# Both MLP products of the second block as seven half-size products of sums of quarters, and a weight ring of four slots

## What is computed

```python
def squared_relu_mlp(h, w_ff1, w_ff2):
    return jnp.square(jax.nn.relu(h @ w_ff1)) @ w_ff2

    for l in range(DEPTH_2):
        ...
        h2 = modulate(rms_norm(x_lat, g_mlp[l]), sh2, sc2)
        x_lat = x_lat + gt2 * squared_relu_mlp(h2, w_ff1[l], w_ff2[l])
```

## Time and profile before

| | |
|---|---|
| three runs, us | 4598.55, 4602.85, 4605.67; median 4602.85 |
| profiled execution, us | 4597.72, its span 4596.0 |
| granted clock of TensorE, mean | 0.928 of 2.4 GHz |
| first MLP product (L342), both layers | 1024 matmuls, 439.9 us |
| second MLP product (L2960), both layers | 1024 matmuls, 439.9 us |
| TensorE / VectorE / ScalarE busy, us | 4005.6 / 1115.7 / 728.0 |

### The profile page before, as it was taken

How to read it: one execution, slowest core, us unless ns; L and a number is a source line. 1 busy time by engine, 2 the same in 40 slices (tenths; PEclk the granted TensorE clock), 3 DMA queues, 4 the chain that set the end, 5 groups by cost and what they waited for, 6 DMA issues and landing times. The chain is left out here.

```text
span 4596.0 us, 36789 instructions
## 1 busy us (share of the span) xinstructions
PE 4005.6 (87%) x14604; PEld 2114.7 (46%) x14604; DVE 1115.7 (24%) x2442; ACT 728.0 (16%) x1623; POOL 166.5 (4%) x374
## 2 busy tenths in 40 slices
PE   8986886997689999999366989999997698989999
PEld 3653853443443445554144554444445455444443
DVE  0148524112222111112224350211001435021000
ACT  0213111000122110001013340110002334010000
POOL 1010000000100000000103000000000300000000
PEclk9987886998699999999688999999998899999999
DMA  7432012223366677887421111222222111221221
GB/s 275 176 127 101 1 41 83 80 85 120 131 267 256 274 296 308 349 315 298 152 61 55 37 37 55 100 83 73 92 68 87 55 37 37 73 110 55 75 103 42
DMA packets 200480, 582.93 MB, mean 127 GB/s; under 512 B 22116, under 2 KB 37780, under 8 KB 187304
## 3 DMA queue, kind: packets, MB, share of 16 engines
q1 hardware_dynamic: 186040, 542.94, 31.9%
q0 software_dynamic: 7184, 23.91, 1.4%
q10 hardware_dynamic: 7088, 13.73, 0.8%
HBM read 545.68 MB, written 34.88 MB: 126 GB/s over the span
## 5 line engine op out<-in xcount | busy, mean ns | idle before, releaser
L342 PE MATMUL ps<-ring,layer_hT 128*128 128x512 f32 (+2 forms) x1632 | 621.1, 540 | 7.9 <-PEq L272 7.9
L342 PEld LDWEIGHTS ps<-ring,layer_hT 128*128 128x128 f32 x1632 | 306.0, 196 | 313.7 <-issue 307.2
L2960 PE MATMUL ps<-ring,mlp_hidden 128*128 128x512 f32 x1024 | 439.9, 592 | 3.2 <-PEq L272 3.2
L342 PE MATMUL ps<-layer_hT,ring 128*128 128x512 f32 x1024 | 439.9, 592 | 1.9 <-PEq L272 1.9
L342 PE MATMUL ps<-ring,mixers_xT 128*128 128x512 f32 (+3 forms) x992 | 372.5, 532 | 9.4 <-DVE ab_qk L336 6.0
L2960 PEld LDWEIGHTS ps<-ring,mlp_hidden 128*128 128x128 f32 x1024 | 194.4, 190 | 248.8 <-issue 248.8
L342 PEld LDWEIGHTS ps<-layer_hT,ring 128*128 128x128 f32 x1024 | 194.4, 190 | 246.3 <-issue 246.3
L342 PEld LDWEIGHTS ps<-ring,mixers_xT 128*128 128x128 f32 x992 | 188.6, 200 | 187.3 <-issue 174.1
L342 PE MATMUL ps<-mixers_xT,ring 128*128 128x512 f32 (+2 forms) x560 | 188.4, 496 | 1.9 <-DMA ring<-in_w_ff 1.0
L2032 PE MATMUL ps<-ring,moe_xgT 128*64 128x512 f32 x320 | 144.4, 607 | 2.9 <-issue 2.9
L342 PEld LDWEIGHTS ps<-mixers_xT,ring 128*128 128x128 f32 (+1 forms) x560 | 104.0, 187 | 84.0 <-issue 74.7
(11 more groups left out here) (734 smaller groups left out, 4974.2 us busy)
## 6 DMA issues: line engine op xcount, KB each, us to landing
ring<-in_w_ff SPq DMA_DIRECT2D x40, 2048.0 KB
ring<-in_w_in SPq DMA_DIRECT2D x33, 2048.0 KB
ring<-in_e_up SPq DMA_DIRECT2D x21, 2048.0 KB
ring<-in_w_ada SPq DMA_DIRECT2D x18, 2048.0 KB
ring<-in_e_down SPq DMA_DIRECT2D x18, 2048.0 KB
ring<-in_e_gate SPq DMA_DIRECT2D x18, 2048.0 KB
ring<-in_w_out SPq DMA_DIRECT2D x8, 2048.0 KB
mixers_ring_more<-in_e_gate SPq DMA_DIRECT2D x8, 2048.0 KB, 9.3
```

What stands on the lines that cost most here:

```text
L342: last = pe.matmul(out, lhsT, rhs, start=(j == 0), stop=(j == len(pairs) - 1))
L2960: last_ = pe.matmul(M.ps[:, bank_of(half, t), :], hidden[:, k * DK + j, t * P:(t + 1) * P], w[:, j, :], start=(k == 0 and j == 0), stop=(k ...
```

## The change

Both products are done in Winograd's form of Strassen's scheme. With A and B cut into quarters (11, 12, 21, 22) the sums are S1 = A21 + A22, S2 = S1 - A11, S3 = A11 - A21, S4 = A12 - S2 and R1 = B12 - B11, R2 = B22 - R1, R3 = B22 - B12, R4 = B21 - R2. The products, by their numbers in the code, are 1 = A11 B11, 2 = A12 B21, 5 = S1 R1, 6 = S2 R2, 7 = S3 R3, 3 = S4 B22 and 4 = A22 R4, issued in this order. The result is C11 = 1 + 2, C12 = 1 + 6 + 5 + 3, C21 = 1 + 6 + 7 + 4 and C22 = 1 + 6 + 7 + 5. All sums are made on VectorE.

*First product* (`first_product`): a pair of weight tiles (1024 x 1024) is A, and `hT` is B, cut at 512 features and 256 tokens. Each of the seven products is two groups (x = 0, 1); a group has 2 x 4 products of 256 moving columns. S of each pair is made on VectorE from the tiles (128 x 2048 elements an operation), R once a layer from `hT` (128 x 1024). ScalarE evacuates products 1 and 5; VectorE evacuates the rest, adds the parts and makes relu and square in one scalar_tensor_tensor. There are four pairs.

*Second product* (`second_product`): a part is 1024 hidden features, with `hidden` as A and two tiles of `w_ff2` (1024 rows x 512 columns each) as B. Each of the seven products is two groups of 4 products with 512 moving columns. The seven products of the four parts are accumulated in SBUF: part 0 is copied there by ScalarE, parts 1 to 3 are added by VectorE. In the last part the results are combined, scaled and added to the rows behind each product. The rows are loaded from ScalarE's queue after part 0, into `hidden`'s space, and each is saved from there as soon as it is done. The sums S are 128 x 1024 elements, R 128 x 2048.

*Ring:* `RING` is 4 and the extra slot of the first block goes, so the first block has four slots and the experts five, as before, and the second block four in place of three. The spare experts' up-weights go to the buffer `loose` of the context instead of a slot. The order of the tiles of `w_ff2` follows the parts.

```diff
-RING = 3
+RING = 4
...
-    wg, wu = M.weights.bufs[RING:RING + 2]
+    wg, wu = M.weights.bufs[RING], loose[:, 0:TILE]
...
-        for half in range(2):
-            for k in range(4):
-                tiles += weight_tiles(A["w_ff2_2"][l, k * D:(k + 1) * D], half * BANK, (half + 1) * BANK)
+        for k in range(4):
+            tiles += weight_tiles(A["w_ff2_2"][l, k * D:(k + 1) * D], 0, D)
...
+def left_sum(i, link, eng, bufs, a11, a12, a21, a22):
+    one, two = bufs
+    if i == 1:
+        return eng.tensor_tensor(one, a21, a22, ALU.add)
+    if i == 2:
+        return eng.tensor_tensor(two, one, a11, ALU.subtract)
+    if i == 3:
+        return eng.tensor_tensor(one, a11, a21, ALU.subtract)
+    return eng.tensor_tensor(two, a12, two, ALU.subtract)
...
+def first_product(M, name, hT, hidden, sums):
...
+    def product(p, x, left, right, ev, on, needs, after=()):
+        def pe(pe_, bank):
+            for h in range(2):
+                c = (2 * x + h) * P
+                last = matmuls(pe_, bank[:, h * rows:(h + 1) * rows],
+                               [(left[:, j, c:c + P], right[:, j, :]) for j in range(half)])
+            return last
...
+    def square(dve, out):
+        return dve.scalar_tensor_tensor(out, out, 0.0, out, ALU.max, ALU.mult)
+
+    def left(p, i, reads, after=()):
+        def ev(dve, _, link):
+            if i == 1:
+                W.arrived(dve, t0 + 2 * p)
+                W.arrived(dve, t0 + 2 * p + 1)
+            return left_sum(i, link, dve, S, *a(p))
+        return group(None, ev, "v", reads=reads, after=after)
...
+        p2 = [product(p, x, a12, b[2], lambda dve, bank, link, p=p, x=x: c11(dve, bank, link, p, x), "v", (),
+                      (p1[x],)) for x in range(2)]
+        p5 = [product(p, x, S[0], R[0], lambda act, bank, link, p=p, x=x: act.activation(
+            dst(p, x, 1, 1), bank, ACT.Copy), "s", (s1, r1)) for x in range(2)]
+        gs += p1 + p2 + p5
+        s3 = left(p, 3, (p5[1],), (s2,))
...
+def second_product(M, name, hidden, hT, gt, sums, last):
...
+        def add(n, x, left, right, needs, then=None, after=()):
+            v = V[n, x]
+
+            def ev(eng, bank, link, k=k):
+                if k == 0:
+                    return move(eng, v, bank)
+                total = eng.tensor_tensor(v, v, bank, ALU.add)
...
+        both("1", a11, b11, ())
+        both("2", a12, b21, (), c11, lambda x: (now["1", x], loaded[x]))
+        both("5", S[0], R[0], (s1, r1))
+        s3, r3 = left(k, 3, (now["5", 1],), (s2,)), right(k, 3, (now["5", 1],), (r2,))
+        gs += [s3, r3]
+        both("6", S[1], R[1], (s2, r2), u2, lambda x: (now["1", x], now["5", x], before["3", x]))
+        s4, r4 = left(k, 4, (now["6", 1],)), right(k, 4, (now["6", 1],))
+        gs += [s4, r4]
+        both("7", S[0], R[0], (s3, r3), c22, lambda x: (now["6", x], before["4", x], loaded[2 + x]))
...
+        both("3", S[1], b22, (s4,), c12, lambda x: (now["6", x],))
...
+        both("4", a22, R[1], (r4,), c21, lambda x: (now["7", x],))
...
 def mlp(M, L, l, hT, last):
...
-        products(M, f"ff1_p{l}", gs, tiles=8)
...
+        first_product(M, f"ff1_{l}", hT, hidden, sums)
+        second_product(M, f"ff2_{l}", hidden, hT, gt, sums, last)
```

More of the change, by code:

```diff
@@ L2024, in experts @@
         sc = st.ctx.enter_context(Stage(nc, "ctx"))
-        sections, load_ctx = context_sections(M, sc, lambda i: index["ctx", i])
+        sections, load_ctx, loose = context_sections(M, sc, lambda i: index["ctx", i])
         filler = by_slot(sections, places, 2 * pairs)
@@ L2108, in experts, with spare_experts @@
             spare_experts(M, sr, route, slot_rows, idx, xg[:, 0, :], xgT[:, 0, :, :], sg[:, 0, :], h[:, 0, :],
[L2109 to L2112 removed]
+                          hT[:, 0, :], y[:, 0, :], loose)
+def spare_experts(M, st, route, slot_rows, idx, xg, xgT, sg, h, hT, y, loose):
     nc, A, sig, ds = M.nc, M.A, st.sig, bass.ds
     done = st.sb("done", [1, 1])
[L2120 removed]
+    wg, wu = M.weights.bufs[RING], loose[:, 0:TILE]
     wd = M.xT[:, :, :].rearrange("p k n -> p (k n)")
@@ L2905, in squared_relu, with right_sum @@
     return ev
+def left_sum(i, link, eng, bufs, a11, a12, a21, a22):
[7 more added lines that the diff above has]
+    return eng.tensor_tensor(two, a12, two, ALU.subtract)
+def right_sum(i, link, eng, bufs, b11, b12, b21, b22):
+    one, two = bufs
+    if i == 1:
+        return eng.tensor_tensor(one, b12, b11, ALU.subtract)
+    if i == 2:
+        return eng.tensor_tensor(two, b22, one, ALU.subtract)
+    if i == 3:
+        return eng.tensor_tensor(one, b22, b12, ALU.subtract)
+    return eng.tensor_tensor(two, b21, two, ALU.subtract)
@@ L2913, in mlp @@
         gt = st.sb("gt", [P, D])
+        sums = st.sb("sums", [P, 9 * BANK * 2])
         products(M, f"gt2_{l}", gate_row_groups(M, L.mod, 5 * DK, 0, gt))
[L2915 to L2919, removed]
-        products(M, f"ff1_p{l}", gs, tiles=8)
-        x = hT[:, :, :].rearrange("p k n -> p (k n)").rearrange("p (t d) -> p t d", d=D)
@@ L2923, in mlp @@
[L2923 to L2959, removed]
-                                last_ = pe.matmul(M.ps[:, bank_of(half, t), :],
-                                                  hidden[:, k * DK + j, t * P:(t + 1) * P], w[:, j, :],
-                                                  start=(k == 0 and j == 0), stop=(k == 3 and j == DK - 1))
-                            if k == 3 and t < TT - 1:
-                                last_.then_inc(sig["summed"], 1)
-                        last_.then_inc(W.groups_done, 1)
-            @block.vector
-            def _(dve):
-                link = Chain(dve, sig["chain"])
-                dve.wait_ge(sig["x"], 16 * TT)
-                for half in range(2):
-                    for t in range(TT):
-                        if t < TT - 1:
-                            dve.wait_ge(sig["summed"], half * (TT - 1) + t + 1)
-                        else:
-                            dve.wait_ge(W.groups_done, base + 4 * half + 4)
-                        ev(dve, M.ps[:, bank_of(half, t), :], link, t, half).then_inc(sig["moved"], 1)
@@ L3231, in context_sections @@
     sections += [ks + nk_work, vs + nk_turned + near_saves]
-    return sections, load
+    return sections, load, ins
 def by_slot(sections, places, slots):
@@ L3321, in program @@
             tiles += [t] + turns[2 * j:2 * j + 2]
-        slots = [RING + 1] * len(tiles)
+        slots = [RING] * len(tiles)
         for n in range(4):
@@ L3362, in program @@
         with Stage(nc, "mixers") as st:
-            M.weights.bufs.append(st.sb("ring_more", [P, TILE])[:, :])
             M.ones = st.sb("ones", [P, P])
```

161 lines of the change are left out of this document (added).

## The result

The changed kernel takes 4484.17 us (median of four runs, 4481.17 to 4488.25) against 4600.7 for the kernel before, run beside it (four runs, 4590.02 to 4605.67): ratio 0.975, 95% interval 0.9731 to 0.977. The forecast was 4491, its range 4479 to 4513. A second set of runs gave 4486.03 (five runs) against 4595.25 (nine runs), ratio 0.9757 (0.9743 to 0.9772). Between the profiled executions, whose terms the forecast added up, the spans went from 4596.0 to 4486.5: -109.5 us, where -111.6 was forecast.

The account below looks back on a forecast made before the run. TensorE bounds both MLP products, by number of matmuls times spacing. Terms -107.9 - 2.1 + 0.4 - 2.0 = -111.6 us against the profiled 4597.72 give 4486.1; with 5.1 to the median, 4491, range 4479 to 4513.

Parts of the forecast that it names:

- First product, -26.5 a layer: First MLP product: 896 matmuls of 256 columns at 0.2158 us, 193.5 us a layer against 219.97.
- Second product, -27.5 a layer: Second MLP product: 448 matmuls of 512 columns at 0.4293 us, 192.5 us a layer against 219.97.
- Seam between the products, +0.2 a layer: Between the MLP products: last evacuation 0.70 + 0.75 us on VectorE, so +0.2 us a layer.
- Sums and evacuations: VectorE in both MLP products: 2.29 us per sum of 2048, about 100 us busy in each, all covered.
- Slack of S4: Sum S4 is ready before product 3 by 3.1 us in the first product, 1.0 in the second's last part.
- Ring, -2.1: Second block's ring of four slots: TensorE's two waits for a ring tile go, -2.1 us in all.
- End of layer 0, -1.5: After layer 0's MLP: next stage's first load issued 9.6 us after the last matmul in place of 11.1, -1.5 us.
- End of layer 1, -0.5: After layer 1's last matmul: 10.3 us to the span's end in place of 10.7, worked out as -0.4 us.
- The barrier, 0 with a bound of +5: Semaphore barrier, 5.2 us each before the MLP: it may move or one may be added, 0, at most +5 us.
- (a): Rival, first product: half-width matmuls run at the slower spacing of L658, +20.4 us, 4511 us; chance 0.06.
- (b): Rival, both products: VectorE late at each hand-over and the tail grows, +15 to +35 us, say 4516; chance 0.09.
- (c): Rival, first product: weight loads not hidden behind half-width matmuls, 0.19 us more for each of 1792, 4831 us; chance 0.02.

Follow-up runs that it names:

- ring of four alone: The kernel before with only the new number of ring slots, both MLP products and the tile order as before: 4594.81 us, ratio 1.0002.
- the kernel without sums: The changed kernel with every sum of quarters on VectorE cut to one element and the products reading plain quarters: 4485.3 us, ratio 0.9759.
- the held tiles: The changed kernel with the last two 1 MB weight tiles of layer 0's MLP loaded only after the row saves: 4480.31 us, again 4479.94 us.
- the strided kernel: The changed kernel with the first product's stationary operand read as every fourth column in place of 128 adjacent ones: 4513.06 us, ratio 0.9824.
- the two tests of S4: The changed kernel with sum S4 made three times over, in the first product (4501.44 us) or in the second (one run, 4489.47 us).

## Why the prediction was right

The mechanism and the main terms held; the terms of the seams and tails were off by 1 to 2 us each. What each step measured:

- **First product, -26.5 a layer.** -26.4 in layer 0: 193.6 us, with the spacing of the context's run. In layer 1 the first run takes 16.11 us in place of 14.05, at a granted clock that the window gives as 0.99 on average: -24.3. The forecast had no term for a start at the low level. The changed kernel's second profile has it the other way round (15.58 in layer 0, 14.05 in layer 1), and the old first product has it too in some traces (ring of four alone: 222.0 and 222.1 us), so this one falls where it falls and costs up to 2 us a time.
- **Second product, -27.5 a layer.** -27.5 and -25.8, the latter again with a slow first run (15.67 for 13.97). This slow start is not by chance alone: it is in layer 1 of seven of the eight kept traces with both new products and in layer 0 of five, and in none of the ten second products of the other five traces. What sets it off the runs don't settle. The idle time just before is 1.99 to 2.44 us in the former (also in the four that start at full clock) and 1.60 to 1.84 in the latter. The sum had no term for it: 1.7 us a time.
- **Seam between the products, +0.2 a layer.** +0.4 and +0.7, so the idle time before the four products is 6.5 us in all, above the "under 5" that was named.
- **Sums and evacuations.** Sums of 2048 elements were forecast at 2.29 us, the additions at 0.70. The groups of the changed kernel in layer 0 (2995 to 3400 us), answering to the earlier trace rows:

```profile
L2968 DVE SCALAR_TENSOR_TENSOR mlp_hidden<-mlp_hidden 128x512 f32<-128x512 f32 x32 | 22.1, 691 | 1.1
L3109 DVE TENSOR_TENSOR layer_hT<-layer_hT,ps 128x512 f32<-128x512 f32 x24 | 16.5, 687 | 43.5 <-PE ps L342 43.5
...
L2917 DVE TENSOR_TENSOR mlp_sums<-ring,mlp_sums 128x2048 f32<-128x2048 f32 x4 | 9.1, 2284 | 0.0
...
L2917 DVE TENSOR_TENSOR mlp_sums<-mlp_hidden,mlp_sums 128x1024 f32<-128x1024 f32 x4 | 4.9, 1220 | 3.4 <-PE ps L342 3.4
```

  VectorE's busy time of about 100 us a product came out as 98.7 and 101.3. "TensorE waits for no sum" is shown by the timeline, and by the kernel without sums.
- **Slack of S4.** VectorE's rows of the two S4's in the changed kernel, the first with the start of product 3 behind it:

```profile
3079.94 2.29 DVE L2917 TENSOR_TENSOR mlp_sums<-ring,mlp_sums 128x2048 f32<-128x2048 f32 x1
3085.24 7.07 PE L342 MATMUL ps<-layer_hT,mlp_sums 128*128 128x256 f32 x32
...
3373.74 1.22 DVE L2917 TENSOR_TENSOR mlp_sums<-mlp_hidden,mlp_sums 128x1024 f32<-128x1024 f32 x1
```

  They end at 3082.23 and 3374.96; product 3 starts at 3085.24 and 3376.51. 3.0 and 1.55 us.
- **Ring, -2.1.** The wait is gone; the gain is within what the runs differ by.
- **End of layer 0, -1.5.** This is the term that was mis-sized most: TensorE's gap went from 26.23 to 26.36, +0.1. The tail was shorter than forecast and the saves slower, for the reason that the held tiles show.
- **End of layer 1, -0.5.** (The forecast works out -0.4 and adds it up as a share of -2.0.) Measured -2.7: 8.0 us from the last matmul to the span's end in place of 10.7. No weight loads are left there beside the saves, which take 4.4 us to landing, and the tail is 3.2 us and not 4.7, since VectorE's additions follow each other every 0.61 to 0.72 us and the last part ran less far behind than a price of 0.73 each makes it.
- **The barrier, 0 with a bound of +5.** It moved, and none was added: -0.15.

The misses nearly cancel: layer 0 gave 2.0 us less than forecast, layer 1 2.2 less, the stretch between them 2.5 more and the one ahead of both 0.3 less. That the sum comes within 2.1 us is thus partly luck: the 2.5 us lie in code where the traces differ by more than that. The 7 us between the forecast and the first median are of another kind: the forecast took the distance of the profiled execution to the median of the kernel before (5 us) over to the changed one, whose profiled execution was the slowest of its four. The three runs of the kernel before, on which the forecast stands, were also high ones: its later medians, 4592.06 to 4595.25, are 8 to 11 us lower.

Of the rivals, (a) had the right mechanism for an operand that this change doesn't have, and its price was too low (20.4 us where the strided kernel's spacing gives 31); (b) is reached only with 3.0 and 1.55 us more work at the two places, as the two tests of S4 show; (c) is refuted by 0.2159 us with 190 ns loads in every matmul. The sentence of the Trainium skill that the prediction quotes with (c) stands in the section The mechanism of its page (TensorE: Matmul & The Clock Gate), one section ahead of the one named; these runs disagree with it as the earlier rows did.

## What to carry to other kernels

Where TensorE runs without a hole, as here, the time of a product is the number of its matmuls times their spacing, and work that trades matmuls for additions on another engine pays in full as long as that engine's queue stays ahead at the tightest hand-over; find that hand-over from the order of the operations, and measure its slack by adding work to it. Take a bound on a spacing from runs of one form only, and the duration of a load from its mean, not from the busy time by the count. A ring with one more slot lets transfers start sooner; look at what else is on the way at that moment, above all saves that the next stage waits for.

## What the runs showed of the hardware

- Reading the stationary operand with a stride of four elements raises a load from 190 to 329 ns. Such loads overlap each other and follow every 0.233 us, more than the 0.216 us of a matmul with 256 columns. With 512 columns (0.429 us) it was not tried.
- Twice as many matmuls of half the width cost 1.28 us for 512 more of them, 2.5 ns each, with every one's 190 ns load hidden.
- VectorE's operations of 512 elements last 0.69 us, but where the second doesn't wait for the first they start 0.61 us apart (3390.83 to 3391.44 above), and 0.72 where it does (3389.39 to 3390.11). A queue of such pairs is shorter than the sum of its durations.
- Four saves of 512 KB took 8.2 us to landing (median) with two 1 MB loads issued among them, and 2.6 without.
- A product of 448 matmuls that starts at a granted clock of 0.50 takes 1.7 us more (194.20 for 192.50); the first 32 carry all of it (15.67 for 13.97).
- Over the first 3000 us, which are the same code, two profiled executions of the changed kernel differed by 8.4 us.
